# A Mamba-2 scan without the product of C and the state in a group's first chunk, and without the state's update in its last

## The reference

```python
cb = jnp.einsum('bclgn,bcsgn->bcgls', cc, bc)
y_diag = jnp.einsum('bcgls,bgrcls,bcsgrp->bclgrp', cb, decay, x_dt)
decay_states = jnp.exp(a_cum[..., -1:] - a_cum)
states = jnp.einsum('bclgn,bgrcl,bclgrp->bcgrpn', bc, decay_states, x_dt)
...
states = jnp.concatenate([jnp.zeros_like(states[:, :1]), states], axis=1)
states = jnp.einsum('bgrzc,bcgrpn->bzgrpn', decay_chunk, states)[:, :-1]
y_off = jnp.einsum('bclgn,bcgrpn,bgrcl->bclgrp', cc, states, jnp.exp(a_cum))
y = (y_diag + y_off).reshape(bsz, seqlen, SSD_HEADS, P)
```

## Time and profile before

| | us |
|---|---|
| median of 3 runs | 1698.18 (1691.99 to 1700.16) |
| the profiled execution | 1699.01 |
| its span, first to last instruction | 1697.3 |

### The profile page before, as it was taken

The page is one execution under the profiler, slowest core; times in us unless marked ns, Lnnn a source line. Parts: engine busy times, 40 slices in busy tenths (PEclk is TensorE's granted clock), DMA queues, the critical chain, the costliest instruction groups (busy, mean ns, idle before and its releaser), DMA issues. The chain is left out here.

```text
span 1697.3 us, 26206 instructions
## 1 busy us (share of the span) xinstructions
PE 1587.0 (94%) x7462; PEld 1282.2 (76%) x7462; DVE 1288.1 (76%) x2319; ACT 709.7 (42%) x1203; POOL 624.5 (37%) x754
## 2 busy tenths in 40 slices
PE   6999999999999999999999883699999999999996
PEld 5778888878888788888888673577777777777774
DVE  6658868768778688687786756578788878888883
ACT  5333232322233232322332330565666566656662
POOL 2222121131221312211302111346767766666674
PEclk9999999999999999999999885799999999999998
DMA  4121121121121211212212635699999999999992
GB/s 152 45 81 46 54 71 37 48 70 44 57 69 44 61 47 52 74 34 54 72 42 62 221 119 199 218 335 363 367 365 378 371 371 369 367 378 364 364 357 80
DMA packets 142991, 292.67 MB, mean 172 GB/s; under 512 B 21340, under 2 KB 71948, under 8 KB 142896
## 3 DMA queue, kind: packets, MB, share of 16 engines
q1 hardware_dynamic: 127904, 266.29, 44.9%
q0 software_dynamic: 14992, 25.22, 4.1%
HBM read 291.81 MB, written 25.30 MB: 187 GB/s over the span
## 5 line engine op out<-in xcount | busy, mean ns | idle before, releaser
L1846 DVE TENSOR_TENSOR gu_lo<-w_gu,gu_hi 128x1024 fp32r<-128x1024 f32 x256 | 308.3, 1225 | 68.5 <-ACT gu_hi L1719 56.7
L1027 PE MATMUL proj<-uTh,wl 128*128 128x512 f32 x768 | 310.9, 405 | 6.7 <-issue 6.7
L1028 PE MATMUL proj<-uTl,wh 128*128 128x512 f32 x768 | 302.9, 394 | 0.0
L1029 PE MATMUL proj<-uTh,wh 128*128 128x512 f32 x768 | 302.7, 394 | 0.0
L1719 ACT ACTIVATE gu_hi<-w_gu 128x1024 fp32r<-128x1024 f32 x256 | 262.7, 1057 | 94.1 <-PE g_ps L1783 40.9
L450 POOL TENSOR_TENSOR wl<-raw,wh 128x512 fp32r<-128x512 f32 x96 | 128.8, 1360 | 388.3 <-ACT wh L511 388.3
L1027 PEld LDWEIGHTS proj<-uTh,wl 128*128 128x128 f32 x768 | 146.4, 191 | 37.4 <-issue 7.3
L1029 PEld LDWEIGHTS proj<-uTh,wh 128*128 128x128 f32 x768 | 146.3, 191 | 32.1
L1028 PEld LDWEIGHTS proj<-uTl,wh 128*128 128x128 f32 x768 | 146.5, 191 | 28.9
L564 ACT ACTIVATE xbc<-v 128x512 f32<-128x512 f32 x64 | 40.5, 633 | 296.0 <-DVE v L847 296.0
L847 DVE SCALAR_TENSOR_TENSOR v<-xr,cw,v 128x512 f32<-128x512 f32 x192 | 146.2, 761 | 15.7 <-DVE v L847 1.5
(11 more groups left out here) (259 smaller groups left out, 3332.9 us busy)
## 6 DMA issues: line engine op xcount, KB each, us to landing
w_gu<-in_moe_w_gate_dram SPq DMA_DIRECT2D x128, 512.0 KB
w_gu<-in_moe_w_up_dram SPq DMA_DIRECT2D x128, 512.0 KB
w_d<-in_moe_w_down_dram SPq DMA_DIRECT2D x128, 512.0 KB
raw<-in_ssd_w_in_dram SPq DMA_DIRECT2D x96, 256.0 KB, 3.4
E<-acum_dram SPq DMA_DIRECT2D x64, 256.0 KB, 3.5
raw<-in_ssd_w_out_dram SPq DMA_DIRECT2D x32, 256.0 KB, 2.9
hacc<-in_x_dram SPq DMA_DIRECT2D x8, 512.0 KB, 7.5
u_dram<-xbc SPq DMA_DIRECT2D x8, 512.0 KB, 2.6
```

Of the source, the lines that this page charges most:

```text
L1027: nc.tensor.matmul(out, al, bh, start=start, stop=False)
L1028: nc.tensor.matmul(out, ah, bl, start=False, stop=False)
L1029: return nc.tensor.matmul(out, ah, bh, start=False, stop=stop)
L1846: vec.tensor_tensor(wl[:, j % RING, :], weights.gate_up(b, j), wh[:, j % RING, :].bitcast(F32), ALU.subtract).then_inc(w_lo, 1)
```

## The change

The counts first: `states`, `sums` and `updates` are the numbers of state products, of steps on `ysb` and of steps on `S` ahead of chunk n, now that a group has 7 of the first, 15 of the second and 13 of the third instead of 8, 16 and 16.

```diff
+        def states(n):
+            return n if n < NT else n - 1
+        def sums(n):
+            return max(2 * n - 1, 0) - (n > NT)
+        def updates(n):
+            return max(2 * n - 1, 0) - 2 * (n >= NT) - (n > NT)
...
             def copy_b(G, c):
+                if c == NT - 1:
+                    return
                 wait(act, tcb_done, G, NT, c + 1)
-                wait(act, st_mm, G, NT, c - 1)
+                wait(act, st_mm, G, NT - 1, states(c - 1))
...
             def prep(G, c):
-                wait(dve, btok_done, G, NT, c + 1)
+                if c == NT - 1:
+                    wait(dve, tcb_done, G, NT, c + 1)
+                else:
+                    wait(dve, btok_done, G, NT - 1, states(c) + 1)
...
-                wait(dve, xdt_steps, G, 2 * NT, 2 * c + 1)
-                wait(dve, st_mm, G, NT, c - 1)
+                if c == NT - 1:
+                    return
+                wait(dve, xdt_steps, G, 2 * NT - 1, c + 1 + states(c))
+                wait(dve, st_mm, G, NT - 1, states(c - 1))
...
-            def y_and_state(G, c, last_chunk):
+            def y_and_state(G, c):
...
-                vec.tensor_tensor(heads(ysb[:]), heads(y_ps[:, 0, :]), spread(eac, G, c), ALU.mult).then_inc(y_steps, 1)
-                wait(dve, y_steps, G, 2 * NT, 2 * c + 1)
-                vec.tensor_tensor(ysb[:], ysb[:], y_ps[:, 1, :], ALU.add).then_inc(y_steps, 1)
+                if c % NT == 0:
+                    vec.tensor_copy(ysb[:], y_ps[:, 1, :]).then_inc(y_steps, 1)
+                else:
+                    vec.tensor_tensor(heads(ysb[:]), heads(y_ps[:, 0, :]), spread(eac, G, c), ALU.mult).then_inc(y_steps, 1)
+                    wait(dve, y_steps, G, 2 * NT - 1, sums(c) + 1)
+                    vec.tensor_tensor(ysb[:], ysb[:], y_ps[:, 1, :], ALU.add).then_inc(y_steps, 1)
+                if c == NT - 1:
+                    return
                 new = S[:, (c + 1) % 2, :]
-                wait(dve, st_mm, G, NT, c + 1)
-                if last_chunk:
-                    for j in range(2):
-                        vec.memset(new[:, j * P:(j + 1) * P], 0.0).then_inc(s_steps, 1)
+                wait(dve, st_mm, G, NT - 1, states(c + 1))
+                if c % NT == 0:
+                    vec.tensor_copy(new, st_ps[:, 0, :]).then_inc(s_steps, 1)
                     return
...
             def scan(G, c):
...
-                wait(pe, s_steps, G, 2 * NT, 2 * c)
-                wait(pe, y_steps, G, 2 * NT, 2 * c)
-                nc.tensor.matmul(y_ps[:, 0, :], xbc[:, H[1] % 2, 3, cc * P:cc * P + P], S[:, c % 2, :], start=True, stop=True)
+                wait(pe, y_steps, G, 2 * NT - 1, sums(c))
+                if cc:
+                    wait(pe, s_steps, G, 2 * NT - 3, updates(c))
+                    nc.tensor.matmul(y_ps[:, 0, :], xbc[:, H[1] % 2, 3, cc * P:cc * P + P], S[:, c % 2, :], start=True, stop=True)
...
+                if c == NT - 1:
+                    return
+                wait(pe, xdt_steps, G, 2 * NT - 1, c + 2 + states(c))
```

More of the change, by code:

```diff
@@ L895, in make_m @@
                 vec.tensor_tensor(E[:, c % 2], E[:, c % 2], cb, ALU.mult).then_inc(m_done, 1)
-            def y_and_state(G, c, last_chunk):
+            def y_and_state(G, c):
                 wait(dve, y_mm, G, NT, c + 1)
                 wait(dve, yT_done, G, NT, c)
-                vec.tensor_tensor(heads(ysb[:]), heads(y_ps[:, 0, :]), spread(eac, G, c), ALU.mult).then_inc(y_steps, 1)
-                wait(dve, y_steps, G, 2 * NT, 2 * c + 1)
-                vec.tensor_tensor(ysb[:], ysb[:], y_ps[:, 1, :], ALU.add).then_inc(y_steps, 1)
+                if c % NT == 0:
[6 more added lines that the diff above has]
+                    return
                 new = S[:, (c + 1) % 2, :]
-                wait(dve, st_mm, G, NT, c + 1)
-                if last_chunk:
-                    for j in range(2):
-                        vec.memset(new[:, j * P:(j + 1) * P], 0.0).then_inc(s_steps, 1)
+                wait(dve, st_mm, G, NT - 1, states(c + 1))
+                if c % NT == 0:
+                    vec.tensor_copy(new, st_ps[:, 0, :]).then_inc(s_steps, 1)
                     return
-                wait(dve, s_steps, G, 2 * NT, 2 * c)
+                wait(dve, s_steps, G, 2 * NT - 3, updates(c))
                 vec.tensor_tensor(heads(new), heads(S[:, c % 2, :]), spread(dch, G, c), ALU.mult).then_inc(s_steps, 1)
-                wait(dve, s_steps, G, 2 * NT, 2 * c + 1)
+                wait(dve, s_steps, G, 2 * NT - 3, updates(c) + 1)
                 vec.tensor_tensor(new, new, st_ps[:, 0, :], ALU.add).then_inc(s_steps, 1)
@@ L961, in _ @@
             prep(G0, 1)
-            y_and_state(G0, 0, False)
+            y_and_state(G0, 0)
             make_m(G0, 1)
@@ L985, in body @@
                     if c < NT or not last:
-                        y_and_state(G, c, c == NT - 1)
+                        y_and_state(G, c)
                     if more:
@@ L1066, in tcb @@
                 wait(pe, unit_final, H, NU, 7 if cc < 4 else 8)
-                wait(pe, xdt_steps, G, 2 * NT, 2 * (c - 1))
-                wait(pe, btok_done, G, NT, c - 1)
+                wait(pe, xdt_steps, G, 2 * NT - 1, 2 * (c - 1))
+                wait(pe, btok_done, G, NT - 1, states(c - 1))
                 out = tcb_ps[c % 2]
@@ L1086, in scan @@
                 mm.then_inc(y_mm, 1)
-                wait(pe, xdt_steps, G, 2 * NT, 2 * c + 2)
-                wait(pe, btok_done, G, NT, c + 1)
+                if c == NT - 1:
+                    return
+                wait(pe, xdt_steps, G, 2 * NT - 1, c + 2 + states(c))
+                wait(pe, btok_done, G, NT - 1, states(c) + 1)
                 wait(pe, gate_steps, G, 24, 3 * c)
@@ L1092, in turn_y @@
             def turn_y(G, c):
-                wait(pe, y_steps, G, 2 * NT, 2 * c + 2)
-                wait(pe, s_steps, G, 2 * NT, 2 * c + 2)
+                wait(pe, y_steps, G, 2 * NT - 1, sums(c + 1))
+                wait(pe, s_steps, G, 2 * NT - 3, updates(c + 1))
                 for t in range(2):
```

## The result

| | before | after |
|---|---|---|
| median, us | 1698.22 (6 runs, 1691.99 to 1700.16) | 1679.65 (6 runs, five of them 1673.59 to 1680.70) |
| ratio | | 0.9885, 95% interval 0.9861 to 0.9908 |
| the profiled execution | 1699.01, span 1697.3 | 1673.59, span 1671.8 |

The changed kernel is 18.6 us (1.1%) faster; one execution here of 4062 us and one in experiment 9 of 1807.58 us were disturbed, and they count in the medians but not in the ratios. The forecast was 1685.8, which is 12.4 us faster, with 1680 as the lower end of its range, so the direction was right and the gain was undersized by a third. Timed again beside later experiments, the changed kernel took 1681.25 us against 1698.58, ratio 0.9892 (0.9875 to 0.9909).

What follows compares the result with a forecast made beforehand. TensorE was taken to bound the grouped scan, its matmuls covering 807.82 of 825 us. Gains 6.2 + 2.9 + 1.2 + 1.7 + 1.2 less 0.8 make 12.4 us: 1698.2 to 1685.8 us, range 1680 to 1695.

Steps and rivals of the forecast that it cites:

- Two 'issue' waits of 3.5 to 3.7 at the loop's branch and no third: Sign for the profile after: TensorE's instruction waits at the loop's branch stay two, 3.5 to 3.7 us.
- a rival that makes the kernel slower: Longer loop body stalls TensorE for instructions, 5.4 us per added stall; chance 0.05, with 0.05 more for one or two.
- TensorE comes there 0.44 earlier, the state two operations of 0.42 earlier, so no new wait: Step 8, at `turn_y(8)`: VectorE does two operations of four, and TensorE gets no new wait for the state.
- VectorE work is free except when it stands ahead of steps 3, 5 or 7: Price of VectorE work in the grouped scan; also excepted were group 0's first chunk and group 7.
- the row of group 4: Step 5's `sum_squares` wait there, 0.58 us against 0.33 in group 6, used to price register instructions.
- Step 7: Groups 0 to 6: a state product of 0.44 us less each, plus 7 x 0.42 = 2.9 us of wait.
- waits for the square: `sum_squares` waited 28 times, 21.0 us in all, for ScalarE's square, in steps 3, 5 and 7.
- group 0's first chunk with its clock: TensorE's idle 2.16 us shrinks by 1.2 us, and the clock's fall behind it goes, 1.7 us.
- the 0.43 for a product: Each TensorE product removed in steps 7 and 8 was forecast at 0.44 us (0.33 to 0.44), 14 x 0.44 = 6.2 us.
- the registers: Five more register instructions per VectorE step cost 12 x 0.07, 0.8 us, in steps 3 and 5 of six groups.
- Group 7's: Step 6's `xdt` wait and `xds` go, and step 7's state product: together 1.2 us (0.6 to 1.3).

Runs made afterwards that it cites:

- experiment 9: The changed kernel with the mean square ahead of `xds` in step 7 on VectorE; 1677.16 us, ratio 0.987 (0.985 to 0.9889).
- Experiment 6: The changed kernel with TensorE waiting, at the loop body's end, until VectorE has made M of the next chunk; 1683.68 us, ratio 0.9906.
- Experiments 4: The kernel before with the first-chunk half of the change only where the loop's branch follows (groups 2, 4, 6); 1692.47 us, ratio 0.9976.
- 5: The kernel before with the first-chunk half only at borders without a branch (groups 1, 3, 5, 7); 1692.32 us, ratio 0.9969.
- experiments 2: The kernel before with the first-chunk half of the change alone, in every group, counts padded; 1684.49 against 1696.68 us, ratio 0.9929.
- 7: The changed kernel with the unread product of C and the state computed again in first chunks of groups 1 to 7; 1685.65 us, ratio 0.9925.
- 10: The changed kernel with padded semaphore counts and the mean square ahead of `xds` together; 1678.16 us, ratio 0.988 (0.9863 to 0.9897).

## Why the prediction fell short

**The step that failed** is "Two 'issue' waits of 3.5 to 3.7 at the loop's branch and no third". There was no third, but the two are 2.4 to 2.5. The forecast had their row and used it only for a rival that makes the kernel slower. It did not ask what sets their length. TensorE's sequencer reaches the branch when `turn_y(8)`'s wait for the state is over, while products of the output projection are still queued; the branch then takes 3.8 to 4.7 us, and TensorE is idle for what the queue doesn't cover. Before, the state stood at 341.28 and the branch began at 341.55, with 0.6 us of matmuls left. After, it began at 334.98, with 2.2 us left. The sum had counted VectorE's two operations in step 8 at nothing ("TensorE comes there 0.44 earlier, the state two operations of 0.42 earlier, so no new wait"). That is right for waits and wrong for the branch, whose idle time fell by 1.31 and 0.97 us. Experiment 6 puts it back. The size was off too: of the two operations that are gone, the multiplication of the state takes 0.84 in the earlier trace rows and 1.00 ahead of the first branch, not 0.42. The Trainium skill ("Runtime: NRT & Kernel Launch", section "Instruction fetch mechanics") says that a taken branch whose target isn't in the window of fetched instructions makes the engine fetch it by DMA before it goes on. The traces agree: TensorE's two long branches are the taken ones, each with its transfer on an instruction queue, and that of the loop's exit takes 0.08 us.

**The clock behind it.** Behind the shorter idle time the clock can stay up, and in this execution that is the larger part, 2.9 and 1.6 us of the 6.8. It isn't sure in a single execution: of 14 idle times between 2.35 and 2.64 us the clock fell behind 4, of the 10 from 2.81 up behind all 10. So the gain at the branches is 2.3 us by the wait, and up to 4.5 by the clock.

**The slack of VectorE in step 8 was not free elsewhere either.** "VectorE work is free except when it stands ahead of steps 3, 5 or 7" left out that step 3 of groups 1, 3 and 5 waited 1.45 to 1.51 and not 0.58. The total of the earlier trace rows had them, the forecast took the row of group 4 for all. Experiments 4 and 5 show where the 2.7 us come from. Nothing in the forecast led to them, and in experiments 2, 5, 7 and 10 the same meeting hit group 0 instead: these 2.7 us are luck, though they repeat with the same program.

**Step 7 was oversized**, 6.0 against 3.2. The two reasons were right: VectorE's chain starts earlier (in step 6 `ysb` starts 8.9 us ahead of step 7's last `tcb` load instead of 8.2) and the wait for the square is gone. But two gains of 0.4 in one step add up only to the next thing that is late, and this was `ms`, 0.50 us. The forecast named waits for the square, not those behind it.

**What held:** group 0's first chunk with its clock (in all eight traces with the copies there TensorE is idle there for 1.15 to 1.16 us, with PEclk 1.00 behind it); the 0.43 for a product; the registers. **Group 7's** 1.2 us can't be told as a whole from the clock's 5.9 us between two executions of one program; 0.4 of them show in the wait for the square in step 7. Put together: 12.4 - 2.8 (step 7) + 6.8 (branches) + 2.7 (step 3) + 0.3 (the small terms) - 1.2 (group 7) = 18.2, and the medians say 18.6. That they agree so well is partly chance, since 4.5 of the 18.2 are clock, and in five of the eight traces with the copies ahead of the branches (experiment 6 aside) it fell behind one branch or both.

## What to carry to other kernels

Where an engine stands idle at a loop's branch, look up when its sequencer reached the branch. A wait just ahead of the branch can cost as much time as the branch is uncovered, even when that wait costs nothing itself. When two savings meet in one step, list what would be the next to be late before adding them. A stretch full of short idle times may hold several us of clock that differ between executions; take no gain there from one trace.

## What was new about the hardware

- A taken branch takes 3.82 to 4.67 us on TensorE's sequencer over the 24 of the table, and it overlaps with matmuls that are already queued. It ends 1.35 to 1.43 us after a transfer of 16384 bytes on an instruction queue; what is short or long is the time until that transfer begins (1.16 to 2.31 us) and the transfer itself (0.93 to 1.38). What delays its beginning stays open.
- The clock may stay up after 2.64 us of idle time and fall after 2.16. In group 0's first chunk it fell in three of the four traces with 2.16 us of idle time (0.60, 0.60, 0.62) and stayed at 1.00 in the fourth. The Trainium skill ("TensorE: Matmul & The Clock Gate", section "What's actually happening") says, of a kernel's start, that the number of slow matmuls differs between runs of the same kernel. These rows fit: the four kernels do the same work up to there.
- `xds` (L907) takes 0.41 us on VectorE in group 0's first chunk and 1.50 us in step 7 of group 0, where GpSimd makes `wl` at the same time. In step 1 of a group the same meeting stretches an operation of 0.42 us to as much as 1.48, and TensorE's wait two steps on from 0.6 to 1.5.
